# Expert weights of a two-block transformer kernel: one 12 KB row a partition in place of 8 KB and 4 KB parts, cast and subtracted at once

## The chip, the cores and the metric

The kernel runs on one core of a Trainium2 chip. The metric is device time in microseconds (us) of one execution. The kernel before took 2507.03 us, the median of three runs (2505.1 to 2518.43). One execution was recorded by the profiler; all rows below are of it.

## The reference

Two transformer blocks of two layers each, on 256 tokens of width 1024, in float32. What matters here is the last feed-forward layer, a mixture of eight experts of width 3584, two for each token:

```
def swiglu_2(t, w_gate, w_up, w_down):
    return (jax.nn.silu(t @ w_gate) * (t @ w_up)) @ w_down

def moe_swiglu(h, router_w, w_gate, w_up, w_down):
    ...
    logits = (t @ router_w).astype(jnp.float32)
    top_v, top_i = lax.top_k(logits, TOP_K)
    top_p = jax.nn.softmax(top_v, axis=-1)
    gates = jnp.sum(jax.nn.one_hot(top_i, N_EXPERTS, dtype=jnp.float32) * top_p[..., None], axis=1)
    ...
    for e in range(N_EXPERTS):
        out = out + gates[:, e:e + 1] * swiglu_2(t, w_gate[e], w_up[e], w_down[e])
```

Before it come the rest of both blocks (attention, a gated linear attention and a state space mixer, three dense feed-forward layers), and after it a last norm. None of that changes.

## The kernel before

All weights pass through a ring of four slots in the on-chip memory (`RING`, `SLOTS = 4`), 12 KB a partition each. A slot has a front of 8 KB (`PART` = 2048 columns of float32) and a back of 4 KB. The sync engine's sequencer (SP) walks a fixed plan of weight pieces; `load_front` (L330) and `load_back` (L336) each issue one DMA, and each waits first until the slot's front or back has been used four pieces earlier (`front_used`, `back_used`).

The hidden width of an expert is cut in 28 chunks of 128, so the stage has 8 x 28 = 224 chunks. For a chunk the front holds 128 columns of the gate and of the up weights (1 MB in all), the back the 128 rows of the down weights (0.5 MB). In DRAM the fronts of all partitions of a chunk stand first, then the backs (`packed_ffn`), so a front is a DMA of 128 rows of 8 KB and a back one of 128 rows of 4 KB.

The matrix engine (PE) multiplies in bf16 with split operands: each float32 weight is a high bf16 part and the rest as a low bf16 part, and three products stand for one. ACT makes the high part by a copy (`cast`), DVE the low part by a subtraction of the high part from the float32 weight; this subtraction is what frees the ring. In `moe_parts` ACT casts a front at L1445 and a back at L1451, DVE subtracts at L1500 and L1505. The gate/up parts of four chunks have their places in three tensors (`turned`, `normed_or_mix`, `ctx_sb`), the down parts of four in `aux`.

Each expert gathers its tokens, at most `CAP = 96` of them. Chunks go in pairs. PE (L1375 to L1377) makes gate and up products of two chunks, 96 matmuls of 96 columns, then the down products of the pair before (L1387 to L1389, 12 matmuls of 512 columns). ACT takes the silu of a pair (L1456), DVE multiplies it with the up product (L1512), ACT casts this hidden product (L1461), DVE subtracts (L1515). When an expert is done, DVE copies its output (L1519), and PE adds it to the sum over experts, put back to the tokens' places (L1395). The order on each engine is written out in `silus`, `gating` and `products`, with loops over groups of four chunks. If an expert has more than 96 tokens, another path runs (`general_parts`); in the recorded run it doesn't.

Ahead of the stage stands the router's block. While it chooses experts, ACT (L960, L2533, L2535) and DVE (L970, L2489, L2491) already split the fronts of chunks 0 and 1 and the back of chunk 0. The blocks are parted by barriers over all engines: SP issues the weights of chunks 4 and on (chunks 0 to 3 are loaded earlier) only when the experts' block has begun.

## Time and profile before

| what | value |
|---|---|
| runs | 2507.03 us median, 2505.1 to 2518.43 |
| the profiled execution | 2505.05 us, its span 2503.3 us |
| PE, DVE, ACT busy | 91%, 74%, 60% of the span |
| granted PE clock, mean | 0.966 |
| DMA traffic | 674.33 MB, 269 GB/s over the span |
| expert stage | about 1634 to 2483 us; 224 chunks of 1.57 MB |

The span is the time from the first to the last instruction of the profiled execution. A busy share is the part of the span in which an engine had an instruction in work. The idle time ahead of an instruction is put down to what came last before it started. The DMA share is the mean of 16 DMA engines; it can exceed 1, as the records of two packets on an engine may overlap a little.

### The profile page before, as it was taken

Reading aid. Unit: us, or ns where it says so; the run is one execution under the profiler, and the core shown is the slowest. Engines: PE = TensorE matmul, PEld = TensorE weight load, DVE = VectorE, ACT = ScalarE, POOL = GpSimd, SP = SyncE. Lnnn points to the kernel's source line nnn. Section 1 sums busy time; section 2 is a strip of 40 time slices with the busy share of each in tenths; the row PEclk is TensorE's granted clock in tenths of the full one; section 3 lists DMA queues with packets and bytes.
Section 4 is the critical chain, followed back from the end, with each engine's and each line's share of the span. In section 5 each row is a group of like instructions: output and inputs, shape, how many; then the busy total and the mean of one; then the engine's idle time right before and its main releaser. Section 6 shows DMA issues by size and latency. Waiting matters only on the chain. (4 is left out here: it accounts for less than half of the span.)

```text
span 2503.3 us, 54795 instructions
## 1 busy us (share of the span) xinstructions
PE 2268.8 (91%) x21306; PEld 1811.3 (72%) x21329; DVE 1844.2 (74%) x2395; ACT 1490.5 (60%) x1959; POOL 14.9 (1%) x12
## 2 busy tenths in 40 slices
PE   6988999998977789999999899889999999999997
PEld 4744789896844468977689786677777777777775
DVE  3267567777346766656677657699999999999997
ACT  3146466564113556544466543588888888888885
POOL 0000000002000000000000000000000000000000
PEclk9979999999988999999999998999999999999999
DMA  7350377775456047754577753389999999999995
GB/s 306 134 218 1 127 269 255 276 278 198 148 228 267 1 165 258 267 193 182 193 271 269 273 174 133 138 346 417 411 417 415 418 418 408 418 417 418 417 417 214
DMA packets 121209, 674.33 MB, mean 269 GB/s; under 512 B 13488, under 2 KB 13968, under 8 KB 67088
## 3 DMA queue, kind: packets, MB, share of 16 engines
q1 hardware_dynamic: 120032, 664.47, 68.2%
q10 hardware_dynamic: 1072, 8.42, 0.8%
q8 instruction: 70, 1.15, 0.2%
q14 instruction: 35, 0.29, 0.0%
HBM read 671.79 MB, written 1.05 MB: 269 GB/s over the span
## 5 line engine op out<-in xcount | busy, mean ns | idle before, releaser
L1181 PE MATMUL ps<-projected_halves,weights_halves 128*128 128x256 f32 x1504 | 364.9, 284 | 0.0
L1181 PEld LDWEIGHTS ps<-projected_halves,weights_halves 128*128 128x128 f32 x1504 | 288.6, 192 | 3.4
L1505 DVE TENSOR_TENSOR aux<-weights,aux 128x1024 bf16<-128x1024 f32 x223 | 271.5, 1218 | 1.4 <-ACT aux L1451 1.4
L1164 DVE SCALAR_TENSOR_TENSOR weights_halves<-normed_or_mix_halves,weights 128x1024 fp32r<-128x1024 f32 (+1 forms) x145 | 222.6, 1537 | 66.3 <-ACT normed_or_mix_halves L1161 66.3
L1500 DVE TENSOR_TENSOR turned<-weights,turned 128x2048 bf16<-128x2048 f32 x112 | 256.4, 2289 | 8.6 <-ACT turned L1445 4.1
L1445 ACT ACTIVATE turned<-weights 128x2048 bf16<-128x2048 f32 x112 | 213.6, 1907 | 54.4 <-DMA weights<-moe 52.1
L1451 ACT ACTIVATE aux<-weights 128x1024 bf16<-128x1024 f32 x223 | 232.1, 1041 | 2.6 <-PE ps L1389 1.8
L1375 PE MATMUL ps<-projected,turned 128*128 (+1 forms) x1792 | 232.9, 207 | 0.0
L1376 PE MATMUL ps<-projected,turned 128*128 (+1 forms) x1792 | 232.9, 207 | 0.0
L1377 PE MATMUL ps<-projected,turned 128*128 (+1 forms) x1792 | 232.9, 207 | 0.0
L837 PE MATMUL ps<-weights_halves,normed_or_mix_halves 128*128 128x512 f32 (+4 forms) x576 | 218.9, 380 | 0.0
L1387 PE MATMUL ps<-aux,probs 128*96 128x512 bf16 x448 | 173.3, 387 | 42.4 <-DVE probs L1515 42.4
L1161 ACT ACTIVATE normed_or_mix_halves<-weights 128x1024 fp32r<-128x1024 f32 (+1 forms) x145 | 188.8, 1304 | 10.9 <-PE ps L1192 10.9
L1180 PE MATMUL ps<-projected_halves,normed_or_mix_halves 128*128 128x256 f32 x752 | 182.5, 284 | 1.5 <-issue 1.5
L1180 PE MATMUL ps<-projected_halves,aux_halves 128*128 128x256 f32 x752 | 182.5, 284 | 0.0
L1376 PEld LDWEIGHTS ps<-projected,turned 128*128 128x128 bf16 x1792 | 175.2, 98 | 6.5
L1375 PEld LDWEIGHTS ps<-projected,turned 128*128 128x128 bf16 x1792 | 175.2, 98 | 5.1
L881 DVE TENSOR_TENSOR weights_halves<-weights,extra_halves 128x948 fp32r<-128x948 f32 (+4 forms) x80 | 92.7, 1165 | 113.8 <-ACT extra_halves L862 113.8
L1377 PEld LDWEIGHTS ps<-projected,turned 128*128 128x128 bf16 x1792 | 175.2, 98 | 0.0
L1388 PE MATMUL ps<-aux,probs 128*96 128x512 bf16 x448 | 170.8, 381 | 0.0
L1389 PE MATMUL ps<-aux,probs 128*96 128x512 bf16 x448 | 170.8, 381 | 0.0
L1190 PE MATMUL ps<-normed_or_mix_halves,probs_halves 128*128 128x512 f32 x376 | 151.0, 402 | 18.9 <-DVE probs_turned_halves L1237 18.5
(381 smaller groups left out, 5796.5 us busy)
## 6 DMA issues: line engine op xcount, KB each, us to landing
weights<-moe SPq DMA_DIRECT2D x224, 1024.0 KB, 8.5
weights<-moe SPq DMA_DIRECT2D x224, 512.0 KB, 6.6
weights<-l_ffn SPq DMA_DIRECT2D x66, 1024.0 KB, 4.8
weights<-ada SPq DMA_DIRECT2D x64, 1024.0 KB, 5.6
weights<-l_ffn SPq DMA_DIRECT2D x66, 512.0 KB, 4.5
weights<-ada SPq DMA_DIRECT2D x64, 512.0 KB, 6.1
weights<-ffn SPq DMA_DIRECT2D x28, 1024.0 KB, 4.8
weights<-w_in SPq DMA_DIRECT2D x24, 948.0 KB, 4.7
```

The source lines that it names most:

```text
L837: pe.matmul(o, h_hi(k)[:, t], lo, start=False, stop=False)
L1161: return act.activation(to, src, ACT.Copy, scale=1 / (LEAD + 1))
L1164: return dve.scalar_tensor_tensor(out=to, in0=lead.bitcast(F32), scalar=-LEAD, in1=src, op0=ALU.mult, op1=ALU.add)
L1180: pe.matmul(out_, w_lead[j % 2][0][:, t:t + PB], h_lead[:, k, :], start=(k == 0), stop=False)
L1181: mm = pe.matmul(out_, ring(RINGR, j, t, t + PB), h_rest[:, k, :], start=False, stop=(k == KD - 1))
L1375: pe.matmul(o, hi[:, t], xh, start=(k == 0), stop=False)
L1376: pe.matmul(o, hi[:, t], xl, start=False, stop=False)
L1377: mm = pe.matmul(o, lo[:, t], xh, start=False, stop=(k == KD - 1))
L1445: act.activation(gu4[j % SLOTS][0], RING[:, slot(j), 0:2 * D], ACT.Copy).then_inc(S.hi_gu.sem, 1)
L1451: act.activation(down4[j % SLOTS][0], RING[:, slot(j), 2 * D:3 * D], ACT.Copy).then_inc(S.hi_d.sem, 1)
L1500: dve.tensor_tensor(gu4[j % SLOTS][1], RING[:, slot(j), 0:2 * D], gu4[j % SLOTS][0], ALU.subtract).then_inc(front_used.sem, 1)
L1505: dve.tensor_tensor(down4[j % SLOTS][1], RING[:, slot(j), 2 * D:3 * D], down4[j % SLOTS][0], ALU.subtract).then_inc(back_used.sem, 1)
```

## The change

The experts' weights are laid out in DRAM as 226 items of 128 rows of 12 KB. A row of item j holds the gate and up columns of chunk j (8 KB) and the down row of chunk j - 2 (4 KB); the numbers of `BEHIND = 2` say how far down is behind. One DMA loads an item. The first two items are loaded without their down part, the last two without their gate/up part. ACT casts all 3072 columns of an item in one instruction (`item_hi`), DVE subtracts them in one (`item_lo`), and that frees the slot; `back_used` and the semaphore `hi_down` are not used in the stage any more. The split weights of four items lie in one new tensor `expert_weights` over `ctx_sb`, `normed_or_mix` and `turned`, and in `aux`. In the router's block SP issues items 4 and 5, and ACT and DVE split the gate/up parts of items 0 and 1, in 8 KB pieces. DVE's order in a pair was front, hidden rest, back, front, back; now it is one item, hidden rest, one item. The path for more tokens is changed in the same way. The other feed-forward layers keep their fronts and backs.

```diff
-FFNS = ("l0_ffn", "l1_ffn", "ffn2", "moe")
+FFNS = ("l0_ffn", "l1_ffn", "ffn2")
+BEHIND = 2
...
+    def feed_experts(sp, n, i, run):
+
+        total = F2 // PB * NE + BEHIND
+        rows = lambda src: src.rearrange("(p w) -> p w", p=PB)
+
+        def load(m, j, src):
+            s = m % SLOTS
+            at = slice(0, PART) if j < BEHIND else slice(PART, SLOT) if j >= total - BEHIND else slice(0, SLOT)
+            sp.dma_start(RING[:, s, at], rows(src)[:, at]).then_inc(front_in[s].sem, 16)
...
+                with sp.Fori(0, groups) as g:
+                    for q in range(SLOTS):
+                        sp.wait_ge(front_used.sem, g * SLOTS + (m + q - SLOTS + 1))
+                        load(m + q, i + j, d["moe"][bass.ds(g * SLOTS + (i + j + q), 1)].rearrange("o n -> (o n)"))
...
+    def item_hi(act, j, m, part=whole, freed_by=None, g=None):
...
+        act.wait_ge(front_in[s].sem, landed if g is None else g * 16 + landed)
+        if freed_by is not None:
+            act.wait_ge(freed_by[0].sem, m + freed_by[1])
+        act.activation(parts[j % SLOTS][0][:, part], RING[:, s, part], ACT.Copy).then_inc(S.hi_gu.sem, 1)
+
+    def item_lo(dve, j, m, part=whole):
...
+        dve.wait_ge(S.hi_gu.sem, m + S.hi_gu.at(1))
+        dve.tensor_tensor(parts[j % SLOTS][1][:, part], RING[:, s, part], parts[j % SLOTS][0][:, part],
+                          ALU.subtract).then_inc(front_used.sem, 1)
...
             def down(j, c, m, start=False, stop=False):
-                pe.wait_ge(back_used.sem, c + (a + 1))
+                pe.wait_ge(front_used.sem, c + (a + 1 + BEHIND))
                 pe.wait_ge(S.act_done.sem, m + S.act_done.at(3))
                 hi, lo = (hid_hl[j // 2 % 2][h][:, j % 2 * CAP:(j % 2 + 1) * CAP] for h in range(2))
-                w_hi, w_lo = down4[j % SLOTS]
+                w_hi, w_lo = parts[(j + BEHIND) % SLOTS]
...
             with act.Fori(1, n // SLOTS - 1) as g:
                 for i in range(2):
                     silu_pair(i, 2 * g + i)
-                    for j in (2 * i + 2, 2 * i + 3):
-                        gate_up(j + 2, g * SLOTS + (j + 2))
-                        if j % 2 == 0:
-                            product_hi(i, 2 * g + i)
-                        down(j, g * SLOTS + j)
+                    item_hi(act, 2 * i + 4, g * SLOTS + (2 * i + 4), freed_by=freed_by_down(), g=g)
+                    product_hi(i, 2 * g + i)
+                    item_hi(act, 2 * i + 5, g * SLOTS + (2 * i + 5), freed_by=freed_by_down(), g=g)
...
-            def four(c, m, kept=None):
+            def four(c, m, kept=None, parts_=(whole,) * 4):
                 for i in range(2):
-                    gate_pair(i, m + i, lambda: gate_up(2 * i + 4, c + (2 * i + 4)))
+                    gate_pair(i, m + i, lambda: item_lo(dve, 2 * i + 3, c + (2 * i + 3), parts_[2 * i]))
                     if i == 0 and kept is not None:
                         keep_output(kept)
-                    down(2 * i + 2, c + (2 * i + 2))
-                    gate_up(2 * i + 5, c + (2 * i + 5))
-                    down(2 * i + 3, c + (2 * i + 3))
+                    if parts_[2 * i + 1] is not None:
+                        item_lo(dve, 2 * i + 4, c + (2 * i + 4), parts_[2 * i + 1])
...
         with nc.Block() as block:
+            @block.sync
+            def _(sp):
+                feed(sp, place.n + SLOTS, place.n + 2 + SLOTS)
...
-                cast_hi(act, 0, 0, 0, free=False)
-                arrived(act, place.n + 1)
-                act.activation(second_gu[0], second, ACT.Copy).then_inc(S.hi_gu.sem, 1)
-                arrived(act, place.n)
-                act.activation(first_down[0], back, ACT.Copy).then_inc(S.hi_d.sem, 1)
+                item_hi(act, 0, 0, gate_up_part)
+                item_hi(act, 1, 1, gate_up_part)
...
-                feed(sp, a + SLOTS, a + n + SLOTS)
+                feed(sp, a + 2 + SLOTS, a + n + BEHIND + SLOTS)
```

DVE at the first chunks of an expert, in the loop over experts, before (weights is the ring; turned, normed_or_mix, ctx_sb and aux take the split weights, probs and probs_turned the hidden product, extra an expert's output):

```order
L1512 TENSOR_TENSOR probs_turned<-probs,ps 128x192 [waits silu_done]
L1499 ISA
L1500 TENSOR_TENSOR normed_or_mix<-weights,normed_or_mix 128x2048 [waits hi_gate_up]
L1514 REGISTER_ALU
L1515 TENSOR_TENSOR probs<-probs_turned,probs 128x192 [waits hidden_hi]
L1518 ISA
L1519 COPY extra<-ps 96x1024 [waits down_done]
L1504 REGISTER_ALU
L1505 TENSOR_TENSOR aux<-weights,aux 128x1024 [waits hi_down]
L1499 REGISTER_ALU
L1500 TENSOR_TENSOR ctx_sb<-weights,ctx_sb 128x2048 [waits hi_gate_up]
L1504 REGISTER_ALU
```

The same place on DVE now:

```order
L1483 TENSOR_TENSOR probs_turned<-probs,ps 128x192 [waits silu_done]
L997 ISA
L998 TENSOR_TENSOR expert_weights<-weights,expert_weights 128x3072 [waits hi_gate_up]
L1485 REGISTER_ALU
L1486 TENSOR_TENSOR probs<-probs_turned,probs 128x192 [waits hidden_hi]
L1489 ISA
L1490 COPY extra<-ps 96x1024 [waits down_done]
L997 REGISTER_ALU
L998 TENSOR_TENSOR expert_weights<-weights,expert_weights 128x3072 [waits hi_gate_up]
```

Between the product and the hidden rest stands a subtraction of 3072 columns in place of 2048, and the pair has two subtractions of weights in place of four.

ACT in its loop over groups of four chunks, the second pair of a group, before:

```order
L1456 ACTIVATE probs<-ps 128x192 [waits product_made]
L1444 REGISTER_ALU [waits slot_front_in1]
L1445 ACTIVATE turned<-weights 128x2048 [waits up_done]
L1459 REGISTER_ALU
L1461 ACTIVATE probs<-probs_turned 128x192 [waits down_done,product_made]
L1451 ACTIVATE aux<-weights 128x1024 [waits down_done,slot_back_in3]
L1444 REGISTER_ALU [waits slot_front_in2]
L1445 ACTIVATE turned<-weights 128x2048 [waits up_done]
L1451 ACTIVATE aux<-weights 128x1024 [waits down_done,slot_back_in0]
```

And now:

```order
L1439 ACTIVATE probs<-ps 128x192 [waits product_made]
L991 REGISTER_ALU [waits slot_front_in1]
L992 ACTIVATE expert_weights<-weights 128x3072 [waits down_done]
L1442 REGISTER_ALU
L1444 ACTIVATE probs<-probs_turned 128x192 [waits down_done,product_made]
L991 REGISTER_ALU [waits slot_front_in2]
L992 ACTIVATE expert_weights<-weights 128x3072 [waits down_done]
```

The hidden cast stands behind a cast of 3072 columns, and every weight cast waits for the down products of the item that had its place, where a front waited for its up products.

## Rows read from the trace of the kernel before

**Rows 1.** The page: busy by engine; bandwidth in 40 slices.

```profile
PE 2268.8 (91%) x21306; PEld 1811.3 (72%) x21329; DVE 1844.2 (74%) x2395; ACT 1490.5 (60%) x1959; POOL 14.9 (1%) x12
...
GB/s 306 134 218 1 127 269 255 276 278 198 148 228 267 1 165 258 267 193 182 193 271 269 273 174 133 138 346 417 411 417 415 418 418 408 418 417 418 417 417 214
```

**Rows 2.** Stretches: busy us (count) by engine, clock, DMA share, GB/s.

```profile
1663.94:2466.05 802.11, 749.87 (x11576) 614.51 (x11575) 785.01 (x644) 663.22 (x637) 0.00 (x0) 1.00 1.02 416
1900.00:2000.00 100.00, 93.38 (x1456) 76.83 (x1454) 98.10 (x82) 82.82 (x81) 0.00 (x0) 1.00 1.02 417
```

**Rows 3.** Timeline of DVE: start us, us, line, operation.

```profile
1612.98 1.22 DVE L2491 TENSOR_TENSOR aux<-weights,aux 128x1024 bf16<-128x1024 f32 x1
...
1642.52 0.35 DVE L1512 TENSOR_TENSOR probs_turned<-probs,ps 128x192 f32<-128x192 f32 x1 [0.69 <-ACT probs L1456]
...
1651.53 2.28 DVE L1500 TENSOR_TENSOR turned<-weights,turned 128x2048 bf16<-128x2048 f32 x1
1653.74 0.35 DVE L1515 TENSOR_TENSOR probs<-probs_turned,probs 128x192 bf16<-128x192 f32 x1
1654.01 1.22 DVE L1505 TENSOR_TENSOR aux<-weights,aux 128x1024 bf16<-128x1024 f32 x1
1655.14 2.28 DVE L1500 TENSOR_TENSOR turned<-weights,turned 128x2048 bf16<-128x2048 f32 x1
...
1658.74 2.28 DVE L1500 TENSOR_TENSOR normed_or_mix<-weights,normed_or_mix 128x2048 bf16<-128x2048 f32 x1
```

**Rows 4.** Waits, 1640 to 2480 us: total us, times, longest.

```profile
ACT turned L1445 <- DMA weights<-moe: 52.1, 85, 2.0
...
PE ps L1387 <- DVE probs L1515: 42.2, 67, 2.0
ACT normed_or_mix L1445 <- DMA weights<-moe: 28.1, 40, 1.2
...
ACT ctx_sb L1445 <- DMA weights<-moe: 21.2, 42, 0.7
```

**Rows 5.** Timeline of ACT, start and end of the stage.

```profile
1634.26 1.91 ACT L1445 ACTIVATE turned<-weights 128x2048 bf16<-128x2048 f32 x1 [2.30 <-PEq L2420]
...
1663.94 1.91 ACT L1445 ACTIVATE turned<-weights 128x2048 bf16<-128x2048 f32 x1 [0.52 <-DMA weights<-moe]
...
2466.05 1.91 ACT L1445 ACTIVATE turned<-weights 128x2048 bf16<-128x2048 f32 x1 [0.71 <-DMA weights<-moe]
```

**Rows 6.** DMA, 1800 to 2300 us: packets, queue's share, issues.

```profile
DMA packets 38088, 208.07 MB, mean 416 GB/s; under 512 B 4235, under 2 KB 4235, under 8 KB 21152
...
q1 hardware_dynamic: 38086, 208.03, 101.6%
...
weights<-moe SPq DMA_DIRECT2D x133, 1024.0 KB, 8.5
weights<-moe SPq DMA_DIRECT2D x132, 512.0 KB, 6.6
```

**Rows 7.** DMA in 598 to 600 us.

```profile
DMA packets 53, 0.84 MB, mean 419 GB/s; under 512 B 1, under 2 KB 1, under 8 KB 2
...
q10 hardware_dynamic: 53, 0.84, 97.7%
```

**Rows 8.** Groups, 1800 to 2300 us: busy us, mean ns, idle before.

```profile
L1505 DVE TENSOR_TENSOR aux<-weights,aux 128x1024 bf16<-128x1024 f32 x132 | 160.7, 1218 | 0.8 <-ACT aux L1451 0.8
L1500 DVE TENSOR_TENSOR turned<-weights,turned 128x2048 bf16<-128x2048 f32 x66 | 151.0, 2289 | 3.1 <-ACT turned L1445 0.6
L1451 ACT ACTIVATE aux<-weights 128x1024 bf16<-128x1024 f32 x132 | 137.5, 1041 | 2.4 <-PE ps L1389 1.8
...
L1445 ACT ACTIVATE turned<-weights 128x2048 bf16<-128x2048 f32 x67 | 127.8, 1907 | 29.4 <-DMA weights<-moe 29.4
...
L1519 DVE COPY extra<-ps 96x1024 f32<-96x1024 f32 x5 | 6.1, 1212 | 0.0
```

**Rows 9.** The page, DMA issues: KB each, us to landing.

```profile
weights<-l_ffn SPq DMA_DIRECT2D x66, 1024.0 KB, 4.8
```

More of the change, by code:

```diff
@@ L1033, in ffn_done, with general_parts @@
             s.done(n + 2)
-        for s in (S.silu_done, S.act_hi, S.hi_gu, S.hi_d):
+        for s in (S.silu_done, S.act_hi):
             s.done(n)
-    def general_parts(x, f, gates, gate=GB):
-        a, n = place.n, f // PB * NE
+    def general_parts(x, gates, gate=GB):
+        a, n, fc = place.n, experts, F2 // PB
         hid = [PS[:, 4 + p, :] for p in range(2)]
@@ L1058, in products @@
             up(0, 0)
[L1059 removed]
+            up(1, 1)
+            with pe.Fori(0, n // SLOTS - 1) as g:
                 for j in range(SLOTS):
[L1061 to L1066 removed]
@@ L1369, in up @@
                 pe.wait_ge(S.act_done.sem, m + S.act_done.at(1))
-                hi, lo = gu4[j % SLOTS]
+                hi, lo = parts[j % SLOTS]
                 for w in range(2):
@@ L1544, in gating @@
                 four(g * SLOTS + e * fc, 2 * g + e * (fc // 2))
-            for i in range(2):
-                gate_pair(i, n // 2 - 2 + i)
-                for j in (2 * i + 2, 2 * i + 3):
-                    if i == 0:
-                        down(j, n - SLOTS + j)
+            four(n - SLOTS, n // 2 - 2, parts_=(whole, down_part, down_part, None))
             keep_output(NE - 1)
```

297 lines of the change are left out of this document (118 added, 179 removed).

## The prediction

> **What bounds the kernel now.** I read the busy shares and the 40 slices first. No engine is full over the span (PE 91%, DVE 74%, ACT 60%), but the bandwidth row falls into two parts: 130 to 280 GB/s up to about 1640 us, and from there to the end a flat 417 or so [rows 1]. The flat part is the stage of the eight experts, a third of the span. The table by stretches shows that three things are nearly full there: the DMA engines (share 1.02), DVE (785.0 of 802.1 us, 98%) and PE (749.9 of 802.1, 93%); ACT has 17% free [rows 2]. DVE's busy sum flatters it, since its records overlap a little: between 1651.53 and 1658.74 it runs without any gap and does a pair of chunks in 7.21 us [rows 3].
>
> Which of these sets the pace is told by the waits. ACT waits for the weights' DMA 52.1 + 28.1 + 21.2 = 101.4 us in that stage, in 167 waits; PE waits for DVE 42.2 us in 67 waits, which is the echo of it; DVE waits for ACT hardly at all by name [rows 4]. The timeline gives the rate: the cast of chunk 10 begins at 1663.94 and that of chunk 222 at 2466.05, both at the end of such a wait: 802.1 us for 212 chunks, 3.784 us each, 7.57 a pair [rows 5]. That is 0.36 us above what DVE needs for a pair and equals 1.573 MB at 416 GB/s. So the stage runs at the DMA rate, with DVE 5% behind it. A change that speeds only DVE or ACT would give nothing; one that speeds the transfers gives up to 5%, until DVE is the bound.
>
> **Larger rows.** In the stage 38,086 packets carry 208.03 MB in 500 us and take 101.6% of 16 engines' time: 8,128 us of engine time, 39.1 ns a KB (1,000 B) [rows 6]. A packet is a row of 8 or 4 KB (6.1 thousand bytes on average), and every transfer adds 16 tiny ones of 4 bytes. After the change a chunk is 128 rows of 12 KB and 16 tiny packets in place of 256 rows and 32 tiny. The trace has no 12 KB row, but it has larger ones on another queue: in 598 to 600 us that queue carries rows of 16 KB and moves 0.84 MB with 97.7% of the engines' time, 31.3 us or 37.2 ns a KB, at 419 GB/s [rows 7]. Continuous, that would be 419 / 0.977 = 429 GB/s against 417. So a row has a fixed part. With time = c + bytes x b, 1/417 and 1/429 at 6.1 and 16.4 thousand bytes differ by c x (1/6144 - 1/16384), and 12 KB lies at 426 to 427 GB/s: 2.2% less time. The bounds: none at all (if the larger rows' better share is only the lack of other traffic in that short stretch), and 4.8% (37.2 against 39.1 taken as it stands). I take 2.2%, since it rests on rates and not on records that overlap. 3.784 x 0.978 = 3.70 us a chunk; over the 213 chunks or so between the two marks 17.7 us.
>
> By the Trainium skill (DMA: Bandwidth & Descriptors, "Why small descriptors are slow") a packet costs about 3 cycles more than its 32-byte beats. By that estimate a mean row of 6,144 bytes (192 beats) loses 1.6% and one of 12,288 bytes 0.8%, so the gain would be 0.8%, some 6 us instead of 17.7. The rows above bear out a fixed part about three times that, so I keep 2.2% and make the page's figure part of a rival.
>
> **Fewer, wider casts and subtractions.** ACT's 1907 + 1041 ns and DVE's 2289 + 1218 ns a chunk become one each of 3072 columns [rows 8]. The step from 1024 to 2048 columns is 866 ns on ACT and 1071 on DVE, so these take 2.77 and 3.36 us: 0.17 and 0.15 less. By starts, DVE's two take 2.21 and 1.13 us [rows 3], the wide one 2.21 + 1.08 = 3.29, and the pair 2 x 3.29 + 2 x 0.27 = 7.12 us. That stays under the new DMA pair of 7.40, so it earns nothing by itself, but it is what lets the faster stream through: at 7.21 DVE would have had 0.19 us left, now it has 0.28. PE idles 6.5% now and would idle about 4.5%. The copy of an expert's output on DVE (once in 14 pairs, 1.21 us [rows 8]) fits into 14 x 0.28 = 3.9 us.
>
> **The ring is coarser.** This is the edit that can cost. A slot was given back in two parts, gate and up after its subtraction, down after its own; now all 12 KB are held through a cast of 2.77 and a subtraction of 3.36 us. I laid out one pair at a pair time P of 7.40, with T the landing of the even item. ACT casts it from T to T+2.8, then takes the hidden part (0.3), waits for the odd item at T+3.7 and casts it to T+6.4. DVE multiplies just before T, subtracts the previous odd item to T+3.1, finishes the hidden rest to T+3.4 and subtracts the even item to T+6.7. The first subtraction frees the slot whose next item must land at T + P + 3.7 = T+11.1, so 8.0 us remain from issue to landing; the second leaves T + 2P - 6.8 = 8.0 as well. A transfer of 1.5 MB takes 3.7 us on the wire, and where the queue isn't full a 1 MB one lands 4.8 us after its issue [rows 9], 2.5 of it bytes, so 2.3 fixed: 6.0 in all. Two microseconds of slack remain, and the stream stays full. Cost taken: 0, plus 1 us in all for the moments when an expert ends and PE adds its output, which delay a release by more than the slack.
>
> **The start and the end.** Two more items are loaded in the router's block, but items 2 and 3 must be cast and subtracted before item 6 can be asked for. ACT starts at 1634.26 [rows 5]; item 2 is done by about 1640.4. Item 3 is subtracted behind the first product, which came at 1642.52 [rows 3] and moves by 0.7 (two wide casts, 2 x 2.77 us, in place of 1.91 + 1.04 + 1.91), so item 7 is asked for at about 1646.8 and lands near 1652.8; three more at 3.7 put item 10 at 1663.9, where it is now. Even. The router's block casts two gate/up parts where it cast two and a down: DVE's 1.22 us at 1612.98 stands in its chain [rows 3] and goes; I take 1.0 off, as PE is busy with filler there (bounds 0 and 1.1). After the last full item a longer cast and subtraction (+1.9 us) stand against two down parts that no longer come behind the last hidden product; I take 0, bounds -1 and +2.
>
> **Sum.** The profiled execution took 2505.05 us: 17.7 + 1.0 - 1.0 off gives 2487.4. The runs' median is 2507.03, 2 us above the profiled one, so I say **2488**.
>
> **Rivals.**
> *A, the row size gives little.* If the rate stays between 417 and 420 GB/s (row 4 KB and up all alike, or the page's 3 cycles), the stage gains 0 to 6 us and the router's 1: 2498 to 2505. For it: the row that shows larger packets is of 2 us only, with 53 packets. Against it: the share and the rate in that row both say the same.
> *B, the coarse ring starves the stream (slower).* Place: SP's queue, whose one instruction per item now waits for the whole slot. If an item needs more than 8.0 us from issue to landing, every microsecond over is spread on four items: 0.25 us a chunk. The turning point, where 3.70 becomes today's 3.784, is 0.34 us over, a landing at 8.3. The gate/up parts land 8.5 us after issue now [rows 6], with other parts queued ahead of them; if that figure were latency and not queue, a chunk would take 3.70 + 0.125 = 3.825 us, 220 of them 9 us more than now, and with the router's 1 us off the time would be 2515. Against it: 4.8 us in a free queue [rows 9].
> *C, the chain ACT to DVE holds the pair at about 7.5 us.* The hidden part's cast now stands behind a 2.77 us cast that itself waits for the DMA, and the hidden rest on DVE waits for it; late items would add gaps on DVE, which has 0.28 us a pair to spare. At 7.5 a pair (0.07 less than now) 107 pairs gain 7.5 us, the router's block 1: 2498.
>
> **How the numbers follow.** Forecast 0.66, A 0.17, C 0.07, B 0.10. The likeliest case alone spans 2483 to 2494 (a gain of 1.6% to 2.7% in the stage, and the ends' bounds). The far bound of 4.8% would meet DVE at 7.12 + 1.21/14 = 7.21 us a pair, 107 x 0.36 = 38 us and 2468; it needs a rate of 436 GB/s, above every long stretch shown, so I leave it out as 1 in 50 of the forecast's share; to hold 8 in 10 the range takes in most of A and C: 2483 to 2504. A difference of 0.5%, about what a measurement of this kernel can tell from none, is 12.5 us, so faster means under 2494.5: 0.66 less a tenth of it for a gain at the low end, 0.60. Within 0.5%: that tenth, A and C, 0.30. Slower: B, 0.10.
>
> **What would show it.** The bandwidth of the expert stage at 425 to 427 GB/s and the packets of a 500 us stretch down from 38,088 to about 19,500; ACT's casts of 12 KB rows still waiting for the DMA; starts of one tile's cast 14.8 us apart (15.1 now); DVE's wide subtraction at 3.36 us; its busy share some 96% or 97%. I am wrong in the row size if the rate stays at 417 with the queue full, and in the ring if the DMA share falls below 1 while SP waits on DVE and ACT on the DMA in the same stretch.

## The result and the profile after

The changed kernel takes 2525.23 us (median of 14 runs, 2513.32 to 2531.89) against 2509.89 us of the kernel before (14 runs, 2503.8 to 2524.0): a ratio of 1.0058, 95% interval 1.0044 to 1.0072. It is slower by 0.6%; the forecast was 2488 us, with a range of 2483 to 2504. The profiled execution took 2517.39 us, 7.8 us under the median of its kernel; its span is 2515.2.

The page of the changed kernel, busy time by engine and bandwidth in 40 slices, answers to [rows 1]:

```profile
PE 2272.1 (90%) x21306; PEld 1806.6 (72%) x21329; DVE 1832.2 (73%) x2173; ACT 1462.1 (58%) x1737; POOL 14.9 (1%) x12
...
GB/s 304 134 217 1 145 273 252 276 274 185 154 230 248 1 204 251 265 187 153 232 267 264 239 223 119 138 380 413 402 398 409 403 424 403 410 408 403 412 404 221
```

The flat 417 of the expert stage has become an uneven 398 to 424. The table by stretches of the changed kernel (columns as in [rows 2]), first from the cast of item 10 to that of item 222, which are the same two marks as in [rows 5]:

```profile
1659.99:2477.66 817.67, 751.03 (x11524) 610.49 (x11523) 773.66 (x432) 635.42 (x424) 0.00 (x0) 1.00 0.99 407
1900.00:2000.00 100.00, 91.36 (x1415) 74.76 (x1414) 93.52 (x53) 76.58 (x51) 0.00 (x0) 1.00 0.99 406
2080.00:2100.00 20.00, 19.48 (x322) 16.16 (x319) 17.46 (x11) 15.85 (x11) 0.00 (x0) 1.00 0.97 372
```

The stage went from 802.1 to 817.7 us for the same 212 chunks. The engines between DMA and PE are less busy than before (DVE 773.7 of 817.7, 95%, in place of 98%), and the DMA share is 0.99 in place of 1.02: nothing is full over the whole stage any more. The granted clock of PE is 1.00 in the stage before and after, so the clock has no part in the loss. The timeline of ACT in the changed kernel (start us, us, line, operation, idle time before it) shows why:

```profile
1659.99 2.76 ACT L992 ACTIVATE expert_weights<-weights 128x3072 bf16<-128x3072 f32 x1 [0.70 <-DMA weights<-moe]
...
2061.30 2.76 ACT L992 ACTIVATE expert_weights<-weights 128x3072 bf16<-128x3072 f32 x1 [0.71 <-DMA weights<-moe]
...
2064.98 2.77 ACT L992 ACTIVATE expert_weights<-weights 128x3072 bf16<-128x3072 f32 x1 [0.67 <-DMA weights<-moe]
...
2068.68 2.77 ACT L992 ACTIVATE expert_weights<-weights 128x3072 bf16<-128x3072 f32 x1 [0.71 <-DMA weights<-moe]
...
2072.36 2.76 ACT L992 ACTIVATE aux<-weights 128x3072 bf16<-128x3072 f32 x1 [0.67 <-DMA weights<-moe]
...
2078.75 2.76 ACT L992 ACTIVATE expert_weights<-weights 128x3072 bf16<-128x3072 f32 x1 [3.40 <-PE ps L1384]
2081.42 0.35 ACT L1444 ACTIVATE probs<-probs_turned 128x192 bf16<-128x192 f32 x1
...
2093.73 2.76 ACT L992 ACTIVATE expert_weights<-weights 128x3072 bf16<-128x3072 f32 x1 [2.06 <-DMA weights<-moe]
...
2097.80 2.77 ACT L992 ACTIVATE expert_weights<-weights 128x3072 bf16<-128x3072 f32 x1 [1.05 <-DMA weights<-moe]
...
2477.66 2.76 ACT L992 ACTIVATE expert_weights<-weights 128x3072 bf16<-128x3072 f32 x1 [0.71 <-DMA weights<-moe]
```

Away from trouble the casts start 3.68 to 3.70 us apart, 3.69 on average, where they were 3.76 to 3.78 apart before. At 3.69 the 212 chunks would take 782.3 us; they took 817.7. So 35.4 us are lost in single pauses. (Pauses here and below are always counted so: the time from item 10 to item 222, less 212 times the quiet interval.) By the starts of all casts, the nine intervals from the new expert's second item on hold 21.4 us of that at the seven changes of expert, 2.1 to 4.0 each; the other 14.0 us lie elsewhere. The split depends on where the nine begin: one item later they hold 25.3 us. The kernel before, at 3.765 us a chunk, loses 3.9 us in all.

One change of expert can be followed around 2072 us. PE (start us, us, line) runs the sum of the old expert's output ahead of the new expert's down products:

```profile
2073.68 0.21 PE L1372 MATMUL ps<-projected,expert_weights 128*128 x1
2073.73 3.69 PE L1390 MATMUL ps<-extra 96*128 x16
2077.25 0.38 PE L1382 MATMUL ps<-expert_weights,probs 128*96 128x512 bf16 x1
```

DVE in the same place, and ahead of it one quiet item:

```profile
2001.60 3.35 DVE L998 TENSOR_TENSOR aux<-weights,aux 128x3072 bf16<-128x3072 f32 x1
...
2072.00 1.21 DVE L1490 COPY extra<-ps 96x1024 f32<-96x1024 f32 x1
...
2081.80 0.36 DVE L1486 TENSOR_TENSOR probs<-probs_turned,probs 128x192 bf16<-128x192 f32 x1 [1.78 <-ACT probs L1444]
```

The wide cast may overwrite its buffer only when the down products that use it are done; these stand behind the 3.5 us of the sum, so it waits 3.40 us (2078.75). The hidden part's cast stands behind it (2081.42), DVE's hidden rest behind that (idle 1.78 us), and behind DVE the subtraction that gives a slot back. SP's issues come at these times (start us, us):

```profile
2064.41 0.33 SPq L397 DMA_DIRECT2D weights<-moe  x1
...
2080.18 0.33 SPq L397 DMA_DIRECT2D weights<-moe  x1
2085.60 0.33 SPq L397 DMA_DIRECT2D weights<-moe  x1
2089.13 0.33 SPq L397 DMA_DIRECT2D weights<-moe  x1
```

One interval is 5.42 us in place of 3.69. The issue at 2085.60 is the fifth behind that at 2064.41, and at 3.69 us each it would have come at 2082.86: it is 2.7 us late. The bandwidth of the changed kernel from 2080 to 2100 us, in slices of 0.5 us:

```profile
GB/s 442 442 393 393 442 369 344 393 393 418 492 393 295 320 123 221 418 369 393 393 393 369 393 344 393 418 418 418 393 320 295 221 246 221 541 442 418 418 418 369
```

It falls to 123 GB/s at 2087, 1.4 us behind the late issue; and the item issued at 2085.60 lands at 2093.73, 8.1 us later (the cast that waits for it starts then), the next one 8.7 us after its issue. The load issued at 2064.41 had landed at 2072.36; five intervals of 3.69 behind that would be 2090.81, so the landing is 2.9 us late. The lateness of the issue has passed to the landing whole. The groups, waits and DMA of the changed kernel, for the stage as a whole; first 1800 to 2300 us by groups (busy us, mean ns, idle before), to be set beside [rows 8]:

```profile
L998 DVE TENSOR_TENSOR expert_weights<-weights,expert_weights 128x3072 bf16<-128x3072 f32 x97 | 325.0, 3351 | 0.0
L992 ACT ACTIVATE expert_weights<-weights 128x3072 bf16<-128x3072 f32 x98 | 270.8, 2763 | 91.0 <-DMA weights<-moe 68.2 <-PE ps L1384 22.7
```

The waits from 1640 to 2480 us (total us, times, longest), as in [rows 4]:

```profile
ACT expert_weights L992 <- DMA weights<-moe: 112.9, 132, 3.1
...
ACT aux L992 <- DMA weights<-moe: 37.9, 50, 3.2
PE ps L1370 <- DVE expert_weights L998: 37.4, 55, 1.7
ACT expert_weights L992 <- PE ps L1384: 36.6, 24, 3.5
...
PE ps L1370 <- DVE aux L998: 29.7, 47, 2.6
DVE probs L1486 <- ACT probs L1444: 26.6, 30, 1.9
```

And the DMA of the changed kernel from 1800 to 2300 us, as in [rows 6]:

```profile
DMA packets 18719, 204.48 MB, mean 409 GB/s; under 512 B 2080, under 2 KB 2080, under 8 KB 2080
...
q1 hardware_dynamic: 18717, 204.44, 99.4%
...
weights<-moe SPq DMA_DIRECT2D x129, 1536.0 KB, 7.9
```

ACT's waits for the DMA rose from 101.4 to 150.8 us, PE's for DVE at the start of its products from 42.2 us (for the hidden rest) to 67.1 us (for an item's weights), and two waits are all but new: ACT for down products (36.6 us, 1.8 before) and DVE for the hidden cast (26.6 us, 0.9 before).

### The profile page after: what moved, and what is told of

Read it like the earlier page. It is cut to its first block and busy times, and to the rows that moved or that the text cites. A ratio compares the mean times of both kernels' runs of the same rounds, so it can differ in the third digit from the quotient of the medians.

```text
span 2515.2 us, 53215 instructions
## 1 busy us (share of the span) xinstructions
PE 2272.1 (90%) x21306; PEld 1806.6 (72%) x21329; DVE 1832.2 (73%) x2173; ACT 1462.1 (58%) x1737; POOL 14.9 (1%) x12
## 5 line engine op out<-in xcount | busy, mean ns | idle before, releaser
L998 DVE TENSOR_TENSOR expert_weights<-weights,expert_weights 128x3072 bf16<-128x3072 f32 (+2 forms) x169 | 563.1, 3332 | 7.1 <-ACT expert_weights L992 7.1
L992 ACT ACTIVATE expert_weights<-weights 128x3072 bf16<-128x3072 f32 (+2 forms) x169 | 464.3, 2748 | 153.5 <-DMA weights<-moe 113.6
L1370 PE MATMUL ps<-projected,expert_weights 128*128 (+1 forms) x2688 | 359.9, 207 | 43.5 <-DVE expert_weights L998 40.3
L1371 PE MATMUL ps<-projected,expert_weights 128*128 (+1 forms) x2688 | 359.0, 206 | 0.0
L1372 PE MATMUL ps<-projected,expert_weights 128*128 (+1 forms) x2688 | 358.9, 206 | 0.0
L1370 PEld LDWEIGHTS ps<-projected,expert_weights 128*128 128x128 bf16 x2688 | 263.3, 98 | 64.0 <-DVE expert_weights L998 47.9
L1371 PEld LDWEIGHTS ps<-projected,expert_weights 128*128 128x128 bf16 x2688 | 263.5, 98 | 12.9
L1372 PEld LDWEIGHTS ps<-projected,expert_weights 128*128 128x128 bf16 x2688 | 263.5, 98 | 0.0
L998 DVE TENSOR_TENSOR aux<-weights,aux 128x3072 bf16<-128x3072 f32 (+2 forms) x57 | 187.8, 3294 | 0.0
L992 ACT ACTIVATE aux<-weights 128x3072 bf16<-128x3072 f32 (+2 forms) x57 | 154.9, 2718 | 37.9 <-DMA weights<-moe 37.9
L866 PE MATMUL ps<-extra_halves,normed_or_mix_halves 128*128 128x512 f32 (+4 forms) x416 | 158.4, 381 | 6.9 <-DVE turned_halves L915 6.9
L892 ACT ACTIVATE extra_halves<-weights 128x948 fp32r<-128x948 f32 (+4 forms) x80 | 78.8, 989 | 145.1 <-PE ps L868 127.3
L868 PE MATMUL ps<-extra_halves,turned_halves 128*128 128x512 f32 (+4 forms) x416 | 156.7, 377 | 0.0
```

What stands on the lines that cost most here:

```text
L866: pe.matmul(o, h_hi(k)[:, t], hi, start=(k == 0), stop=False)
L868: mm = pe.matmul(o, h_lo(k)[:, t], hi, start=False, stop=(k == KD - 1))
L992: act.activation(parts[j % SLOTS][0][:, part], RING[:, s, part], ACT.Copy).then_inc(S.hi_gu.sem, 1)
L998: dve.tensor_tensor(parts[j % SLOTS][1][:, part], RING[:, s, part], parts[j % SLOTS][0][:, part], ALU.subtract).then_inc(front_used.sem, 1)
L1370: pe.matmul(o, hi[:, t], xh, start=(k == 0), stop=False)
L1371: pe.matmul(o, hi[:, t], xl, start=False, stop=False)
```

## The experiments

All ran beside the kernel before, whose medians were 2507.27 (e1 to e4), 2507.1 (e5 to e8), 2508.28 (e9 to e12) and 2507.37 us (e13 to e16).

**e1: 12 KB rows in the old order.**

```diff
 # the kernel before, with: one DMA an item, rows of 12 KB, BEHIND = 2
+    sp.wait_ge(front_used.sem, g * SLOTS + (m + q - SLOTS + 1))
+    sp.wait_ge(back_used.sem, g * SLOTS + (m + q - SLOTS + 1))
+    load(m + q, i + j, d["moe"][...])
 # casts, subtractions, buffers and order as before
-    act.activation(down4[j % SLOTS][0], RING[:, slot(j), 2 * D:3 * D], ACT.Copy)
+    act.activation(down4[j % SLOTS][0], RING[:, slot(j + BEHIND), 2 * D:3 * D], ACT.Copy)
```

> The kernel before with one thing of the change alone: items of 12 KB rows (chunk j's gate and up, chunk j - 2's down), one DMA each; casts, subtractions, their places and their order on ACT, DVE and PE stay as before, in 8 KB and 4 KB pieces, and a slot is given back when both have been subtracted. Theory of the order (the rows themselves pay, and the changed kernel loses it to what now stands behind what at the end of an expert): 3.69 us an item in the steady part and 28 items in 103.3 us, so 17 us less than before, ratio 0.993. Rival of the slot (a slot held whole is what starves the stream, whatever the order): 3.69 us in the steady part but gaps after each expert as in the changed kernel, ratio 1.000 to 1.006. Rival of the rows (12 KB rows bring slow packets that stop the stream): 1.000 to 1.006 too, with intervals of over 4 us away from the ends of experts.

Measured: 2505.72 us (2498.11 to 2511.19), ratio 0.9982 [0.9963, 1.0000]. Neither expectation is met: the theory wanted 0.993, the rivals 1.000 or more. The slot is given back as a whole here too, so that alone isn't the loss of 0.6%. The quiet rate is 3.69 us as in the changed kernel, and the changes of expert cost 1.1 to 2.8 us each, 12.6 in all. The stage takes 800.5 us, of which 18.2 are pauses; the kernel before has 3.9. So e1 comes out even with the kernel before only because what its rows gain it loses again in pauses. How long is a slot held? ACT's cast in e1 starts, and DVE's last subtraction of the same item runs:

```profile
1999.97 1.91 ACT L1478 ACTIVATE turned<-weights 128x2048 bf16<-128x2048 f32 x1 [0.59 <-DMA weights<-moe]
```

```profile
2004.39 1.22 DVE L1539 TENSOR_TENSOR aux<-weights,aux 128x1024 bf16<-128x1024 f32 x1
```

5.6 us, against 6.6 in the changed kernel, where ACT's record of the item that DVE subtracts at 2001.60 is this:

```profile
1998.32 2.76 ACT L992 ACTIVATE aux<-weights 128x3072 bf16<-128x3072 f32 x1 [0.65 <-DMA weights<-moe]
```

In a ring of four at 3.69 us an item a slot comes round every 14.76 us; what the holding leaves is the time from issue to landing: 9.1 us in e1, 8.1 in the changed kernel. The medians from issue to landing in 1800 to 2300 us say the same:

```profile
weights<-moe SPq DMA_DIRECT2D x132, 1536.0 KB, 8.8
```

8.8 in e1, 7.9 in the changed kernel: the old order has 0.9 us more of the queue filled ahead.

**e2: two loads an item in the changed order.**

```diff
-    sp.dma_start(RING[:, s, at], rows(src)[:, at]).then_inc(front_in[s].sem, 16)
+    sp.dma_start(RING[:, s, 0:PART], rows(src)[:, 0:PART]).then_inc(front_in[s].sem, 16)
+    sp.dma_start(RING[:, s, PART:SLOT], rows(src)[:, PART:SLOT]).then_inc(back_in[s].sem, 16)
```

> The changed kernel with each item loaded by two DMAs, rows of 8 KB and of 4 KB, out of the same layout; everything else as changed. Theory of the order: the steady item goes back to 3.76 us and the gaps at the ends of experts stay at some 4 us each or shrink a little, since the stream is slower: 5 to 20 us over the changed kernel, ratio to before 1.008 to 1.014. Rival of the rows: the gaps go with the rows, and it comes back to the kernel before, 0.998 to 1.002. Rival of the slot: as the theory of the order.

Measured: 2530.57 us (2524.43 to 2540.6), ratio 1.0082 [1.0051, 1.0112]. The quiet rate is back at 3.76 us and the pauses stay (32.3 us). The layout in DRAM is that of the changed kernel, so it is the size of the rows and not their place that sets the rate, and the pauses don't come from it.

**e3: the hidden part's cast ahead of the pair's first item; e4: the sum behind the new expert's first two down products.**

```diff
 # e3, ACT
     silu_pair(i, 2 * g + i)
-    item_hi(act, 2 * i + 4, ...)
     product_hi(i, 2 * g + i)
+    item_hi(act, 2 * i + 4, ...)
     item_hi(act, 2 * i + 5, ...)
 # e4, PE
-    if begins and i == 0 and not first:
-        scatter(e - 1)
+    if late:
+        pe.wait_ge(expert_kept.sem, e)
     for j in (2 * i, 2 * i + 1):
         down(j, ...)
+    if late:
+        scatter(e - 1)
```

> The changed kernel with ACT's cast of the hidden product moved ahead of the first weight cast of its pair (silu, hidden, item, item in place of silu, item, hidden, item). Theory of the order: DVE no longer waits for the hidden cast behind a weight cast that waits itself (26.6 us in 30 waits), but ACT's weight cast at the end of an expert still waits for the down products: 5 to 12 us under the changed kernel, ratio to before 1.001 to 1.004. Rival of the slot and of the rows: no difference from the changed kernel, 1.004 to 1.007.

> The changed kernel with PE's 16 matmuls that add an expert's output moved behind the next expert's first two down products (they stood ahead of them). Theory of the order: ACT's weight cast at the end of an expert waits for these down products 3.4 us in seven places; with the sum behind them the wait falls under 1 us and the 28 items go from some 108 to 104 us: 15 to 25 us under the changed kernel, ratio to before 0.996 to 1.000. Rival of the slot: half of it at most, 1.002 to 1.005. Rival of the rows: no difference, 1.004 to 1.007.

Measured: e3 2518.46 us (2511.64 to 2531.21), 1.0042 [1.0022, 1.0061]; e4 2514.81 us (2509.37 to 2525.88), 1.0032 [1.0010, 1.0053]. Each takes away more than half of ACT's wait for the down products (36.6 us in the changed kernel); in e3 and in e4, 1640 to 2480 us, it is

```profile
ACT expert_weights L992 <- PE ps L1384: 15.0, 11, 1.9
```

```profile
ACT expert_weights L992 <- PE ps L1384: 13.8, 16, 1.2
```

but neither reaches the kernel before. For e4 the theory of the order had wanted 1.000 or less; 1.0032 lies in the range named for the slot. In e3 ACT waits 56.0 us for DVE's product instead.

**e5: no copy and no sum between experts.** The output of the experts but the last is left out.

```diff
-    if begins and i == 0 and not first:
-        scatter(e - 1)
-    if i == 0 and kept is not None:
-        keep_output(kept)
```

> The changed kernel that leaves out, between experts, DVE's copy of an expert's output and PE's 16 matmuls that add it (the last expert's alone are done). If the ends of experts hold the loss: every item 3.69 us, all intervals alike, 1.1 us of DVE and 3.5 us of PE gone in seven places, and 25 to 35 us under the changed kernel, ratio to before 0.992 to 0.997. If slow packets or the whole slot by itself hold it: gaps stay all through the experts, at most 10 us under, 1.002 or more.

Measured: 2498.54 us (2492.82 to 2511.14), 0.9969 [0.9951, 0.9987]; 422 GB/s from 1700 to 2400 us. The stage takes 792.0 us, and its pauses are 9.7 us in place of 35.4. Without the two disturbances the changed order gains. So the changes of expert, with what follows from them later, are where most of the time goes. Seven copies of 1.21 us on DVE and seven sums of 3.5 us on PE are gone as well, so this is the most that moving them could bring in this order; single pauses of 0.3 to 1.3 us are still there.

**e6: as e4, with the copy on ACT.** Hidden cast, then the 128x1024 copy, then the pair's second item.

> The changed kernel with the sum later (as in the run before) and the copy of an expert's output on ACT, behind its cast of the hidden product, in place of DVE. Theory of the order: DVE, which needs 7.1 of the stream's 7.4 us a pair, no longer falls behind by 1.1 us at the end of an expert: 28 items in 103.5 to 105 us, ratio to before 0.993 to 0.998. Rival of the slot (delays of any origin are kept since a slot is held whole): 1.000 to 1.003.

Measured: 2519.21 us (2509.08 to 2526.39), 1.0041 [1.0023, 1.0060]: no better than e4, and the expectation missed. That a delay on ACT reaches the slots in this order as one on DVE does would explain it, but this wasn't measured by itself.

**e7: e1 with the sum later; e8: e7 with the copy on ACT.** The edits are those of e4 and e6, in the old order; the copy stands behind the down cast of the pair's first item.

> 12 KB rows with the order of before, and the sum behind the first two down products. If the wait on PE made the one late item after each expert in the first of these runs (intervals of 4.1 to 6.2 us, some 2.5 us an expert over 103.3), it falls: 5 to 15 us under that run, ratio to before 0.992 to 0.996. If DVE's copy makes it: no difference, 0.997 to 0.999.

> The same with the copy of the output on ACT as well. Both theories of the order's parts: the stream never pauses, 28 items in 103.3 to 103.8 us, 16 to 18 us under before, ratio 0.993. Rival of the slot: gaps stay, 0.996 to 0.999.

Measured: e7 2491.07 us (2488.83 to 2492.88), 0.9927 [0.9904, 0.9951]; e8 2486.38 us (2481.95 to 2495.77), 0.9918 [0.9891, 0.9945], the best version of all. Items 10 and 222 of e8, and its DMA from 1800 to 2300 us:

```profile
1661.21 1.91 ACT L1481 ACTIVATE turned<-weights 128x2048 bf16<-128x2048 f32 x1 [0.61 <-DMA weights<-moe]
...
2445.26 1.91 ACT L1481 ACTIVATE turned<-weights 128x2048 bf16<-128x2048 f32 x1 [0.61 <-DMA weights<-moe]
```

```profile
q1 hardware_dynamic: 19476, 212.69, 100.8%
...
weights<-moe SPq DMA_DIRECT2D x136, 1536.0 KB, 8.8
```

784.1 us for 212 chunks, 3.698 each, of which 1.8 us are pauses; the forecast for the stage was 212 x 3.70 = 784.4 us.

**e9: the two edits in the kernel before, with its 8 and 4 KB rows.**

> The kernel before with its 8 and 4 KB rows, its order and its ring, and with the two edits of the last run alone: the 16 matmuls of the sum behind the next expert's first two down products, and the copy of an expert's output on ACT. It is the control for the ratio of 0.9918. Theory (12 KB rows give 2% in the rate, and the two edits only let the stream run through the ends of the experts): before, 28 items take 105.4 us, ends included, so nothing is lost there and the two edits can give nothing: ratio 0.998 to 1.001, 28 items 105.2 to 105.6 us, 417 GB/s. Rival (the two edits are what brought the gain, and the rows little): ratio 0.994 to 0.996, 28 items near 104 us.

Measured: 2502.02 us (2494.95 to 2511.95), 0.9979 [0.9966, 0.9992]. Items 10 and 222 of e9:

```profile
1663.69 1.91 ACT L1448 ACTIVATE turned<-weights 128x2048 bf16<-128x2048 f32 x1 [0.54 <-DMA weights<-moe]
...
2463.80 1.91 ACT L1448 ACTIVATE turned<-weights 128x2048 bf16<-128x2048 f32 x1 [0.71 <-DMA weights<-moe]
```

800.1 us, against 784.1 with 12 KB rows: the row size is worth 16.0 us, and by the ratios 0.9918 / 0.9979 = 0.994, 15 us. The two edits alone give 2.0 us of the stage (800.1 against 802.1) and, by the ratio, a little more.

**e10: narrow casts and subtractions in the changed order.**

```diff
+    for piece, by, told in ((gate_up_part, freed_by_up(), S.hi_gu), (down_part, freed_by_down(), S.hi_d)):
+        act.wait_ge(by[0].sem, m + by[1])
+        act.activation(parts[j % SLOTS][0][:, piece], RING[:, s, piece], ACT.Copy).then_inc(told.sem, 1)
 # and so DVE's subtractions; the slot is given back behind the second
```

> The changed kernel in its own order, item by item, but each cast and each subtraction in two pieces of 2048 and 1024 columns. The cast's first piece waits only for the up products that use its buffer, the second for the down products; the slot is given back after the second subtraction. Theory that the loss is in the order (DVE subtracts items 2m+3 and 2m+4 beside pair m, one item later than the old order, so that a delay reaches the slots at once): the gaps at the ends of experts stay, ratio 1.004 to 1.008, 28 items 106.5 to 109 us. Rival (the width: a cast of 2.77 us that waits for down products and holds up the hidden cast): the gaps go, ratio 0.998 to 1.001, ACT's waits for PE under 10 us in 1640 to 2480.

Measured: 2525.07 us (2520.37 to 2529.28), 1.0057 [1.0042, 1.0071], the same as the changed kernel's 1.0058, although the casts' waits for PE fall from 36.6 us to 7.8. In this order the width of the instructions costs nothing and earns nothing that these runs could tell. Its profiled execution took 2528.34 us, 10.9 more than that of the changed kernel, and has 44.3 us of pauses: single executions of one order differ by that much, and only the ratios compare the two kernels.

**e11: wide, DVE one item ahead; e12: the same with the sum later.**

```diff
 # DVE beside pair m: product, item, hidden rest, item
-    items 2m+3 and 2m+4
+    items 2m+4 and 2m+5
```

> The changed kernel with wide casts and subtractions, but on DVE item 2m+4 behind the product of pair m and item 2m+5 behind its hidden rest (one item more ahead than in the changed kernel, as the old order had it). Theory of the order: each slot comes free sooner after its cast and PE doesn't wait for DVE at the start of a pair; the ends of experts cost 1 to 2 us in place of 4 to 6; ratio 0.998 to 1.002. Rival (width): the hidden rest on DVE now stands behind a subtraction that itself waits for a cast, so pairs are drawn out and the loss stays or grows: ratio 1.004 to 1.012, with new waits of DVE for ACT over 50 us.

> As the run before, and with the 16 matmuls of the sum behind the next expert's first two down products. Theory of the order: both edits that give reserve together bring the wide form near the old order with the sum later (0.9927): ratio 0.993 to 0.997, 28 items 104 to 105 us. Rival (width): no better than the changed order with the sum later, 1.002 to 1.006.

Measured: e11 2595.41 us (2590.29 to 2601.99), 1.0343 [1.0325, 1.0361]; e12 2585.36 us (2576.6 to 2587.75), 1.0296 [1.0278, 1.0315]. Both expectations missed by far, the rival's in size too. The waits of e11, 1640 to 2480 us:

```profile
ACT expert_weights L992 <- PE ps L1384: 248.4, 99, 8.3
DVE expert_weights L998 <- ACT expert_weights L992: 119.8, 100, 6.2
...
PE ps L1382 <- DVE probs L1486: 106.6, 92, 3.1
```

This is a closed chain: the wide cast waits for down products, DVE's subtraction for the cast, the hidden rest for the subtraction, and the down products for the hidden rest. With wide instructions the early order can't be had, since gate and up weights, whose old buffer has long been free, must wait for the down part's.

**e13 to e16** went on from e10. **e13: narrow, DVE one item ahead** (the edit of e11 on e10). **e14: narrow, the hidden cast between the two pieces of the pair's first item, DVE as in the changed kernel. e15: e13 with the sum later. e16: e1 with one swap on DVE**:

```diff
-    down(2 * i + 2, c + (2 * i + 2))
     gate_up(2 * i + 5, c + (2 * i + 5))
+    down(2 * i + 2, c + (2 * i + 2))
     down(2 * i + 3, c + (2 * i + 3))
```

> The changed kernel with casts and subtractions in two pieces (1.0057), and on DVE item 2m+4 behind the product of pair m and item 2m+5 behind its hidden rest, in place of 2m+3 and 2m+4. ACT's order is as it was. Theory that DVE's lag of one item costs the reserve (in the changed kernel a slot is held 6.6 us from its cast's start to the end of its subtraction, cast at 1998.32, subtracted until 2004.95; in the old order 5.4 to 5.6): the hold falls under 6 us, landings come 8.5 to 9 us after issue, ratio 0.996 to 1.001. Rival (the hidden part's cast behind the whole item is what costs): the hidden rest on DVE now also stands behind a whole item, so the ratio stays at 1.004 or more.

> The changed kernel with casts and subtractions in two pieces (1.0057), and on ACT the hidden part's cast between the two pieces of the pair's first item, as in the old order. DVE's order is as it was. Theory of DVE's lag: the hold stays near 6.6 us and landings at 7.9 to 8.2, ratio 1.003 to 1.006. Rival (hidden part's cast): DVE's waits for ACT go and the ratio comes to 0.998 to 1.001.

> As e13, and the 16 matmuls of the sum behind the next expert's first two down products. Theory of DVE's lag: near the old order with the sum later (0.9927): 0.992 to 0.996, 28 items 104 to 105 us. Rival (hidden part's cast): 1.000 to 1.004, since the hidden rest comes late in every pair.

> The old order with 12 KB rows (0.998) and one swap on DVE: the down subtraction of the pair's first item stands behind the gate/up subtraction of its second item, so this slot is held 2.2 us longer (some 7.8 us in place of 5.6), the other as long as before. No instruction is added or widened and no product gets its weights late. Theory that the time for which a slot is held decides what a one-off delay costs: the mean hold of 6.6 us is that of the changed kernel, so the gaps at the ends of experts come back, 28 items 107 to 109 us, ratio 1.003 to 1.008. Rival (the loss comes from the changed kernel's chain of waits between the engines and not from the ring): 0.996 to 1.000, as in the old order.

Measured: e13 2504.12 us (2497.58 to 2514.07), 0.9986 [0.9971, 1.0002]. e14 2520.84 us (2511.78 to 2524.88 and one execution of 5979.42, which the ratio leaves out; the median of the other five is 2518.14), 1.0051 [1.0032, 1.0071]. Moving DVE's subtractions one item ahead takes the loss against the kernel before away; moving the hidden cast doesn't. The pauses of e13 are 17.9 us, about those of e1, so they aren't gone. The DMA of e13, 1800 to 2300 us:

```profile
DMA packets 19069, 208.22 MB, mean 416 GB/s; under 512 B 2125, under 2 KB 2125, under 8 KB 2125
...
weights<-moe SPq DMA_DIRECT2D x132, 1536.0 KB, 9.1
```

The landing comes 9.1 us after the issue, in place of 8.2 in e10 and 8.1 in e14.

e15 took 2506.05 us (2492.82 to 2515.13), 0.9995 [0.9981, 1.0009], where 0.992 to 0.996 was expected: the sum later gains nothing here, though it gained 0.5% in the old order (e1 to e7). Its pauses are 18.7 us, as many as in e13. In e15 ACT waits 38.7 us for PE before the silu, in e13 23.4. Why the two orders differ in this was not settled.

e16 took 2642.69 us (2639.34 to 2648.19), 1.0548 [1.0533, 1.0562]; 1.003 to 1.008 was expected. The direction is that of the theory and the size isn't: the swap also gives the two slots back 1.1 us apart, so that their loads run together and nothing is loaded in between. The DMA of e16 from 1998 to 2014 us, in slices of 0.4 us, the cast of the slot's item before, and the one cast that waits there:

```profile
GB/s 430 430 215 246 61 31 154 154 123 369 307 338 369 338 399 399 369 215 369 399 338 399 461 338 461 430 430 307 338 215 307 430 338 369 338 369 246 154 399 399
```

```profile
1990.45 1.91 ACT L1478 ACTIVATE normed_or_mix<-weights 128x2048 bf16<-128x2048 f32 x1 [2.83 <-DMA weights<-moe]
...
2008.77 1.91 ACT L1478 ACTIVATE normed_or_mix<-weights 128x2048 bf16<-128x2048 f32 x1 [3.59 <-DMA weights<-moe]
```

Its load was issued at 1999.69 on a queue that had all but run dry: 2 us pass until bandwidth rises, and it lands 9.1 us after its issue. The expectation had this slot held some 7.8 us, which would leave 14.76 - 7.8 = 7.0 us. In the trace it is held longer, 9.2 us from the cast at 1990.45 to the issue at 1999.69, since its last subtraction now stands behind that of the pair's second item, which must first land and be cast. So e16 lengthens the hold, but it also ties one slot's release to the landing of the next item, and doesn't measure the hold by itself.

## Why the prediction was wrong

**What bounds the kernel: right.** The stage ran at the DMA's rate before, and it is the DMA's pauses that count after. In the quiet stretches the items already follow each other at the full rate, so a pause is not made good later.

**Larger rows: right.** Forecast 3.70 us a chunk; measured 3.69 in quiet stretches and 3.698 over the stage of e8, e2 takes it back, and e8 against e9 puts it at 16 us where 17.7 was forecast. The packets halved, 18,719 in 500 us. By the Trainium skill (DMA: Bandwidth & Descriptors, "Why small descriptors are slow") 3 cycles a packet would, by the prediction's estimate, have given 0.8%; 3.765 to 3.69 is 2.0%, so the measurement bears out the larger fixed part of the row and not the page's.

**Wide casts and subtractions: right.** Forecast 2.77 and 3.36 us, measured 2.763 and 3.351. e10 shows that their width has no effect by itself.

**The ring: this is the step that failed.** The prediction said: "Two microseconds of slack remain, and the stream stays full. Cost taken: 0, plus 1 us in all for the moments when an expert ends". The 8.0 us from issue to landing were right (7.9 measured, and 8.1 by the holding time). The slack of two was not there: at the change of expert followed above, an issue 2.7 us late gave a landing 2.9 us late, where two microseconds of slack would have left 0.7. What was wrong in it is the 6.0 us that a load was said to need. They came from a 1 MB load of another stage [rows 9] and bytes at the full rate, as for a load that has the DMA engines to itself. In the stream it shares them with its neighbours: the late load took 8.1 us in the changed kernel (1.57 MB in 8.1 us is 194 GB/s, while 372 were moved in all), and 9.1 in e16. How long a 12 KB-row load would take alone, no run shows. The cost was 35.4 us of lost stream in place of about 1. 25.7 us of it go with the copy and the sum (e5, which keeps 9.7). The hand schedule also had two delays at a change of expert too small, by leaving out that the wide cast now waits behind the sum's 3.5 us (3.40 us of idle ACT) and that the hidden cast stands behind it.

The coarser slot was taken to cost nothing, and here the loss has two parts. The first is DVE's order: e13 differs from e10 by one item on DVE, the time from issue to landing goes from 8.2 to 9.1 us, and 1.0057 falls to 0.9986. The changed kernel subtracts an item only shortly before the next is cast. This lag follows from the wide form: e11 shows that without it the chain closes over the down part's buffer. The second part is left in e1 and e13 too: 18 us of pauses, against 3.9 before. They go when the copy and the sum are moved in the old order (8.7 us in e7, 1.8 in e8), but what makes them, the slot given back whole or the faster stream behind the same engines, was not parted: no run has the old order, whole slots and rows of 8 and 4 KB.

**The start and the end.** Item 10 is cast 4.0 us earlier than before, where 1.0 was forecast, but that is three things. ACT's first cast in the router's block and its first in the experts' block, before and then in the changed kernel:

```profile
1606.62 1.91 ACT L960 ACTIVATE normed_or_mix<-weights 128x2048 bf16<-128x2048 f32 x1 [0.93 <-PEq L573]
```

```profile
1600.55 1.91 ACT L992 ACTIVATE expert_weights<-weights 128x2048 bf16<-128x2048 f32 x1 [0.93 <-PEq L603]
...
1626.72 5.42 ACT L992 ACTIVATE expert_weights<-weights 128x3072 bf16<-128x3072 f32 x2 [2.30 <-PEq L2380]
```

Before, the experts' block starts at 1634.26 [rows 5]. The 6.1 us ahead of the router's block lie in stages that the change doesn't touch, and the same mark scatters from 1600.55 to 1608.96 over the profiled executions. The router's block takes 26.2 us in place of 27.6: 1.5 off where 1.0 was taken, and again 26.2 in e2, e4, e5 and e6. From the first cast of the experts' block to that of item 10 it takes 33.3 us in place of 29.7: 3.6 more where "Even" was forecast, and 32.1 to 34.2 in e2, e4, e5 and e6. The load of item 9, issued at 1646.61, lands at 1656.30, 9.7 us later: here too a load in the stream takes longer than the 6.0 us of a load alone. The end, from item 222 to the end of the span, takes 37.5 us against 37.3: 0 was taken.

**The sum** closes with the measured terms: 2505.05 + 15.6 (stage) - 4.0 (start) + 0.3 (end) = 2517.0, against 2517.39 in the profiled execution. Without the 6.1 us that the change didn't make, the terms add up to 18.0 us; the medians of 14 runs differ by 15.3. The forecast was 17.7 us of gain in the stage; at the quiet rate the gain is there, and 35.4 us of pauses were paid in place of 3.9.

**The rivals.** A is refuted by the rate. B named the right place and the right quantity, issue to landing, and gave 2515; it assumed that every item would come late. In fact the quiet items kept 3.69 us, and only disturbed ones were late; even so the time came out above B's 2515. Its chance of 0.10 was too low: the argument against it was the same 6.0 us. C's waits are there (DVE for the hidden cast, 26.6 us), but e3 and e14 show that removing them brings the ratio only to 1.0042 and 1.0051.

Not settled: what starts the pauses that e5 keeps (9.7 us), what makes the 18 us of e1 and e13, and why the sum later is worth 0.5% in the old order and nothing in e15.

## What to carry to other kernels

When a stream through a ring is the bound, compare the time that the ring leaves from issue to landing (slots x period, less the time a slot is held, from the cast's start to the end of its last reader) with what a load of that size takes when it is issued late in the running stream, measured there, and not with a load alone or with its bytes at full rate. Then list the one-off events (an output copied, a sum added), for what the reserve doesn't cover becomes a pause; in the changed kernel 2.7 us of delay became 2.9. Moving two such events off the path was worth 0.6% with the large rows (e1 to e8) and 0.2% with the small ones (e9).

## What the runs showed of the hardware

- Rows of 12 KB in place of 8 and 4 KB: 3.69 against 3.765 us for 1.57 MB, 426 against 418 GB/s. The packed traces have the time of every packet; its median from 1800 to 2300 us is 160 ns for 4 KB and 314 for 8 KB before, 460 for 12 KB in the changed kernel: 14 ns less for the same bytes. At 128 rows on 16 engines that is an estimate of 0.11 us a chunk.
- The mean DMA share over some tens of microseconds stays near 1 while bandwidth falls: 0.97 at 372 GB/s from 2080 to 2100 us in the changed kernel. The mean packet of 12 KB takes 491 ns there, against 464 from 2060 to 2080 us. GB/s in short slices shows the pauses.
- After a late issue a 1.5 MB load took 8.1 us in the changed kernel and 9.1 in e16, of which 3.7 are bytes at the full rate. By the Trainium skill (DMA: Bandwidth & Descriptors, "Latency and other measured facts") the fixed cost of a DMA is about 2 us. From the late issue to the return of bandwidth it took 2.4 us in the changed kernel (2085.60 to 2088.0) and 1.9 in e16 (1999.69 to 2001.6), which agrees. The rest, some 2 to 3.5 us, isn't shown to be a fixed cost: in both cases the next load followed and shared the engines.
